# Rotary rotation in a Trainium2 decoder kernel: row blocks swapped by DMA inside SBUF instead of a TensorE permutation

## What is computed

```python
def rope(x, pos):                       # x: (..., 64)
    half = QK_ROPE // 2                 # 32
    ...
    x1, x2 = xf[..., :half], xf[..., half:]
    return jnp.concatenate([x1 * cos - x2 * sin, x2 * cos + x1 * sin], axis=-1)

cq = rms_norm(h @ w_dq, q_g)            # 1024 -> 512
q = (cq @ w_uq).reshape(n, t, N_HEADS, QK_NOPE + QK_ROPE)
q_pe = rope(q[..., QK_NOPE:], pos)
```

## Time and profile before

| | |
|---|---|
| median of 3 runs | 1427.34 us (1426.62 to 1427.58) |
| the profiled execution's own time | 1420.13 us |
| its span in the profile | 1417.3 us |
| granted TensorE clock, mean | 0.996 of full speed |
| TensorE busy | 1379.9 us, 97% of the span |
| VectorE busy | 890.2 us, 63% |
| ScalarE busy | 539.3 us, 38% |
| GpSimd busy | 176.0 us, 12% |

### The profile page before, as it was taken

How to read it: one execution, slowest core, us unless ns; L and a number is a source line. 1 busy time by engine, 2 the same in 40 slices (tenths; PEclk the granted TensorE clock), 3 DMA queues, 4 the chain that set the end, 5 groups by cost and what they waited for, 6 DMA issues and landing times.

```text
span 1417.3 us, 30501 instructions
## 1 busy us (share of the span) xinstructions
PE 1379.9 (97%) x11819; PEld 1303.4 (92%) x11819; DVE 890.2 (63%) x1516; ACT 539.3 (38%) x881; POOL 176.0 (12%) x339
## 2 busy tenths in 40 slices
PE   7999999999999999999999989999999999999998
PEld 6999999998999999999989955458999999999997
DVE  4444665226888888833366587674678888884334
ACT  5445444236332222233366132444642222223334
POOL 2000000000222222210000121100021222221000
PEclk9999999999999999999999999999999999999999
DMA  7432222222333333233333565301323333323322
GB/s 230 116 89 75 66 79 78 84 82 76 89 89 92 96 93 89 63 98 92 97 90 105 223 253 184 90 1 46 90 62 103 89 89 93 97 69 89 93 86 76
DMA packets 224442, 138.22 MB, mean 98 GB/s; under 512 B 12710, under 2 KB 220742, under 8 KB 223328
## 3 DMA queue, kind: packets, MB, share of 16 engines
q1 hardware_dynamic: 219688, 112.38, 27.6%
q0 software_dynamic: 4512, 24.69, 4.6%
q10 hardware_dynamic: 168, 0.11, 0.0%
HBM read 133.84 MB, written 3.67 MB: 97 GB/s over the span
## 4 chain that ended last, share of the span: by engine, by line
PE 90%; DVE 4%; ACT 3%; issue 2%; DMA 0%; ACTq 0%; DVEq 0%
PE psum L698 77%; PE psum L1124 2%; PE psum L1256 1%; PE psum L1281 1%; PE psum L1107 1%; PE psum L1085 1%; PE psum L889 1%; DVE kt L2175 1%; PE psum L1259 1%; DVE x L1838 1%; DVE ut L1832 1%; PE psum L875 1%; PE psum L1270 0%; ACT xh L1467 0%; DMA xs<-in_x_prompt 0%
## 5 line engine op out<-in xcount | busy, mean ns | idle before, releaser
L1794 DVE TENSOR_TENSOR wl<-ws,wh 128x1024 fp32r<-128x1024 f32 x214 | 262.0, 1224 | 318.0 <-ACT wh L1341 175.9
L698 PE MATMUL psum<-xh,wh 128*128 128x260 f32 x2032 | 418.6, 285 | 3.4 <-DVE xl L1813 2.7
L698 PE MATMUL psum<-xh,wl 128*128 128x260 f32 x2032 | 415.0, 283 | 0.0
L698 PE MATMUL psum<-xl,wh 128*128 128x260 f32 x2032 | 414.5, 283 | 0.0
L698 PEld LDWEIGHTS psum<-xh,wh 128*128 128x128 f32 x2032 | 316.3, 189 | 6.0 <-issue 3.0
L698 PEld LDWEIGHTS psum<-xh,wl 128*128 128x128 f32 x2032 | 316.0, 189 | 0.0
L698 PEld LDWEIGHTS psum<-xl,wh 128*128 128x128 f32 x2032 | 315.3, 189 | 0.1
L1341 ACT ACTIVATE wh<-ws 128x1024 fp32r<-128x1024 f32 x144 | 152.0, 1056 | 300.4 <-PE psum L698 300.4
L698 PE MATMUL psum<-acth,wh 128*128 128x260 f32 x704 | 145.3, 284 | 0.0
L698 PE MATMUL psum<-acth,wl 128*128 128x260 f32 x704 | 144.1, 282 | 0.0
L698 PE MATMUL psum<-actl,wh 128*128 128x260 f32 x704 | 144.0, 282 | 0.0
(11 more groups left out here) (321 smaller groups left out, 1805.8 us busy)
## 6 DMA issues: line engine op xcount, KB each, us to landing
ws<-in_w_up SPq DMA_DIRECT2D x88, 512.0 KB, 3.8
ws<-in_w_in_a SPq DMA_DIRECT2D x32, 512.0 KB, 4.1
ws<-in_w_down SPq DMA_DIRECT2D x28, 384.0 KB, 3.4
ws<-in_w_down SPq DMA_DIRECT2D x32, 320.0 KB, 3.1
ws<-in_w_out_a SPq DMA_DIRECT2D x16, 512.0 KB, 3.8
ws<-in_w_o SPq DMA_DIRECT2D x8, 512.0 KB, 4.4
xn<-in_x_prompt SPq DMA_DIRECT2D x4, 512.0 KB, 7.8
ws<-in_w_dq SPq DMA_DIRECT2D x4, 512.0 KB, 5.5
```

Of the source, the lines that this page charges most:

```text
L698: mm = pe.matmul(psum[:, 2 * slot + b, 0:HB], w, r[:, k, b * HB:(b + 1) * HB], start=st, stop=en)
L1794: dve.tensor_tensor(low_, ws[:, slot4, :], f32(high), ALU.subtract).then_inc(w_low, 1)
```

## The change

The permutation by TensorE is gone. ScalarE starts transfers from SBUF to SBUF instead, four for each 128-row tile, each of 32 rows of 520 values (2080 bytes a row), from the block of rows beside the one it writes. The sign of the sine goes into the constant table. `rotate` multiplies the swapped copy by the signed sine in place and adds the product of the original with the cosine; all three of its operations now read SBUF. The sums for the query norm move from ahead of the first query tile to a place inside it, ahead of its last quarter. The mask `keep` takes the place of `perm` in the constants, which are 128 columns narrower.

```diff
-    for m in range(P):
-        d = m % ROPE
-
-        c[m + half if d < half else m - half, P + m] = -1.0 if d < half else 1.0
+    c[:, P:2 * P] = np.arange(P)[:, None] <= np.arange(P)[None, :]
...
-    c[:, 3 * P + T:3 * P + 2 * T] = np.tile(np.sin(ang), (4, 1))
+    c[:, 3 * P + T:3 * P + 2 * T] = np.tile(np.sin(ang), (4, 1)) * np.where(np.arange(P) % ROPE < half, -1, 1)[:, None]
...
 # TensorE
-            pe.wait_ge(evac_kv, 3)
-            for b in range(2):
-                mm = pe.matmul(psum[:, 4 + b, 0:HB], perm, krr[:, b * HB:(b + 1) * HB], start=True, stop=True)
-            mm.then_inc(rotk_done, 1)
-            rms("cq")
-
-            def turn_q(t):
...
                 for k in range(KQ):
                     if t == 0:
+                        if k == KQ - 1:
+                            rms("cq")
                         pe.wait_ge(cql_ready, k + 1)
...
-                if 4 <= t < 8:
-                    turn_q(t - 4)
                 if t == 10:
 
                     pe.wait_ge(d_uk, 16)
-                    pe.wait_ge(rotq_step, 8)
+                    pe.wait_ge(ln_done, SSB["cq"] + 1)
...
 # ScalarE
+            def swap_halves(dst, src, sent):
+
+                for lo in range(0, P, ROPE // 2):
+                    act.dma_start(dst[lo:lo + ROPE // 2, :], src[lo ^ (ROPE // 2):(lo ^ (ROPE // 2)) + ROPE // 2, :]).then_inc(sent, 16)
+
             roots()
             rms("kv", r2)
+            act.wait_ge(evac_kv, 3)
+            swap_halves(krt, krr, d_swapk)
...
             rms("cq", r2)
+            def swap_query(t):
+
+                act.wait_ge(evac_uq, t + 1)
+                wait(act, d_swapq[t % 2], 64 * (t // 2))
+                swap_halves(qr[:, t, :], qrr[:, t, :], d_swapq[t % 2])
+
             for j in range(-1, 4):
                 ahead_static(U_UQ + j)
+                if j < 2:
+                    for t in ((0,), (1, 2), (3,))[j + 1]:
+                        swap_query(t)
...
 # VectorE
-            def rotate(dst, raw_, rot, tmp, done, step, n):
-
-                dve.wait_ge(done, n + 1)
-                dve.tensor_tensor(halves(tmp), rot, halves(sin), ALU.mult)
-                dve.tensor_tensor(dst, raw_, cos, ALU.mult).then_inc(step, 1)
+            def rotate(dst, raw_, tmp, sem, value, step, n):
+
+                dve.wait_ge(sem, value)
+                dve.tensor_tensor(dst, dst, sin, ALU.mult)
+                dve.tensor_tensor(tmp, raw_, cos, ALU.mult).then_inc(step, 1)
...
-            rotate(krt[:, :], krr[:, :], psum[:, 4:6, 0:HB], ut[:, 0, :], rotk_done, rotk_step, 0)
+            rotate(krt[:, :], krr[:, :], ut[:, 0, :], d_swapk, 64, rotk_step, 0)
...
-                    rotate(qr[:, j, :], qrr[:, j, :], psum[:, 4 + 2 * (j % 2):6 + 2 * (j % 2), 0:HB], ut[:, j % 2, :], rotq_done, rotq_step, j)
+                    rotate(qr[:, j, :], qrr[:, j, :], ut[:, j % 2, :], d_swapq[j % 2], 64 * (j // 2 + 1), rotq_step, j)
```

More of the change, by code:

```diff
@@ L75 @@
 SSB = {n: sum(2 if m in ON_PE + HALVED else 1 for m, _, _ in GROUPS_SQ[:i]) for i, (n, _, _) in enumerate(GROUPS_SQ)}
-K_SELH = 4 * P + 2 * T + NS
+K_SELH = 3 * P + 2 * T + NS
 K_GRP = K_SELH + H
@@ L129, in constants @@
     c[:, 3 * P:3 * P + T] = np.tile(np.cos(ang), (4, 1))
-    c[:, 3 * P + T:3 * P + 2 * T] = np.tile(np.sin(ang), (4, 1))
+    c[:, 3 * P + T:3 * P + 2 * T] = np.tile(np.sin(ang), (4, 1)) * np.where(np.arange(P) % ROPE < half, -1, 1)[:, None]
     for r in range(NS * H):
         c[r, 3 * P + 2 * T + r // H] = 1.0
-    c[:, 3 * P + 2 * T + NS:4 * P + 2 * T + NS] = np.arange(P)[:, None] <= np.arange(P)[None, :]
     p = np.arange(P)
@@ L227, in trunk @@
         arena = top[0]
-        ident, perm = cst[:, 0:P], cst[:, P:2 * P]
+        ident, keep = cst[:, 0:P], cst[:, P:2 * P]
         cmask = cst[:, 2 * P:3 * P]
@@ L231, in trunk @@
         own = cst[:, 3 * P + 2 * T:3 * P + 2 * T + NS]
-        keep = cst[:, 3 * P + 2 * T + NS:4 * P + 2 * T + NS]
         selh, grp = cst[:, K_SELH:K_SELH + H], cst[:, K_GRP:K_GRP + GRP]
@@ L364, in trunk @@
         csT_done, csn_ready, csn_sent, m_ready = S("csT_done"), S("csn_ready"), S("csn_sent"), S("m_ready")
[L366 to L369, removed]
+        evac_kv, evac_dq, evac_uq, d_swapk, rotk_step, ck_step, ckt_ready = (S(n) for n in (
+            "evac_kv", "evac_dq", "evac_uq", "d_swapk", "rotk_step", "ck_step", "ckt_ready"))
+        cqh_ready, cql_ready, rotq_step = (S(n) for n in ("cqh_ready", "cql_ready", "rotq_step"))
+        d_swapq = [S(f"d_swapq{i}") for i in range(2)]
         ql_read, qlT_done, ols_ready, olpT_done, oss_ready, osT_done, own_low, narrow_clear = (S(n) for n in (
```

## The result

| | before | after |
|---|---|---|
| median, both kernels run in turn, 9 runs each | 1427.18 us (1425.13 to 1428.80) | 1430.97 us (1429.29 to 1432.92) |
| ratio | | 1.0028, 95% interval 1.0019 to 1.0037 |
| the profiled execution, its own time | 1420.13 us | 1432.09 us |
| its span | 1417.3 us | 1430.3 us |

The changed kernel is slower by 4.0 us (0.0028 x 1427), with 2.7 to 5.3 as the interval. 1428.0 was forecast, with 1425.2 to 1431.6 as the range. The time lies in the range, but beyond the 0.2% that the prediction counts as no change. So the forecast was 3.0 us too low, the measured time is 0.6 us inside the range's upper end, and the likeliest case (no change, 0.68) was not the one that came.

The account below looks back on a forecast made before the run. TensorE, busy 97% of the span, was taken to bound the kernel; it gets about 5 us ahead but gives it back before tile 10, which starts 0.7 us later: 1427.34 + 0.7 = 1428.0 us, range 1425.2 to 1431.6.

Parts of the forecast that it names:

- what is removed: TensorE's query tiles: five permutations, 4.35 us, plus a 0.91 us wait, 5.26 us; about 4.9 us gain after a 0.3 us wait.
- what comes late next: Before tile 10: weights of `U_UQ` + 5, queued behind the gathers, land at 805.2, so tile 10 starts at 810.2, 0.7 us later.
- the size of the swaps' addition: Weights of `U_UQ` + 5: swap bytes on the shared DMA engines, 2.5 us at 430 GB/s, delay their landing by 2.1 us.
- the bound of 5: Upper bound in us for the swaps' delay of the weights: twice the bytes' time, if 32-row blocks move at half rate.
- Rival C: DMA: transfers of 32 rows run at half rate, adding 5 us; tile 10 3.7 us later, 1431.0 us, slower; chance 0.08.
- ScalarE behind the swaps: ScalarE's queue: waits for swap landings hold later high parts; decides only if swap 1 lands past 797.2; 794.5 taken.
- rival B: ScalarE held by swaps, swap 1 landing at 800 to 803: tile 10 3.5 to 6.5 us later, about 1432; chance 0.13.
- The chain of 13.0: From swap 1's landing through ScalarE's starts, high and low parts, rotations and tile readings to tile 8's reading: 13.0 us together.
- D: Before tile 10: weights land early enough once TensorE asks earlier; full 4.9 us gain, 1422.4 us, faster; chance 0.11.
- A: Before tile 10: swaps cost the weights nothing, landing stays at 803.1; gain is the cap, 1.4 us, 1425.9; chance 0.18.

Follow-up runs that it names:

- e4: Changed kernel with one more wait: GpSimd starts the gathers only when the last query swap has landed; 1421.79 us against 1426.46, ratio to before 0.9965.
- e5: e3 with the gathers also held until query tile 4 is read; ratio to the kernel before 0.9974.
- e3: Changed kernel without its 20 swap transfers, the rotation reading unswapped rows (results not the reference's); ratio to the kernel before 1.0003.
- e8: As e7, but each query transfer moves 32 of 520 columns and the queries' rotation reads unswapped rows; ratio to the kernel before 1.0007.
- e9: e3 with ten filler matmuls on TensorE ahead of query tile 10, on another chip than most runs; ratio to the kernel before 0.9989.
- e1: The kernel before, profiled once more without any edit; one run, 1428.17 us.
- e7: Changed kernel with own semaphores for query swaps 2 and 3, so ScalarE starts them without waiting for swaps 0 and 1; ratio to before 1.0053.
- e6: The kernel before, with the gathers held until VectorE has read the fifth query tile, on another chip than most runs; ratio to before 1.0003.

## Why the prediction was right or wrong

**Right: what is removed.** 4.9 us were to be gained if nothing came late. e4 and e5 gain 4.95 and 4.94.

**Right: what comes late next.** That the weights of `U_UQ` + 5 set tile 10, that the permutations' gain is given back in front of it, and the order behind them: the high part at 806.67 + 5.0 gives 811.67; tile 10 starts at 811.61. The gathers started at 777.36, which is 779.34 with the shift of 1.98, as forecast. ScalarE's high part is released by the DMA, as was to be seen.

**Wrong: the size of the swaps' addition, "2.1, most of the full sum, since 430 GB/s is a busy state".** From the start of the stretch to the last high part it is 806.67 - 771.76 = 34.91 us. It is 29.36 before, where TensorE releases this high part, and 28.92 in e3, where the weights do. So the addition is 5.5 to 6.0 us. That is the term that was mis-sized, and it lies outside of the bound of 5.

Where it comes from is in the windows from the weights' start to their landing, 27.6 us after and 22.3 us in e3. The shares are means of 16 engines:

- The swaps' own packets are 12.1% of 27.6, 3.3 us.
- The gathers' 720 packets take 73.8% of 27.6 = 20.4 us, against 81.5% of 22.3 = 18.2 in e3 (and 79.1% of 23 = 18.2 before, window 779:802). They are 2.2 us slower beside the swaps.
- The weights' own packets take 7.9% of 27.6, against 7.9% of 22.3 in e3: 0.4 us more.

Together that is 6.0. In e8, with the same packets and a sixteenth of the bytes, nearly all of it is gone (29.34 against the 28.92 of e3). So two things were wrong. The swaps' rows were priced at the rate of the gathers, 2.5 us and 2.1 taken, and they took 3.3: 104 ns a row of 2080 bytes, 20 GB/s per engine, where a gather's packet of 15.4 KB took 577 ns, 27 GB/s. And what the swaps do to the packets of the other queues, 2.6 us, was put at nothing; it is the larger part. Why those packets get slower is open. In e4, where no gathers run, the rows' share is higher still, 31.3% x 16 x 14 us = 70 us of engine time, 137 ns a row or 15 GB/s per engine; that too is not explained.

Rival C had this size (5) and this time (1431.0), with a chance of 0.08. That its time was met is luck in part: it had all of the 5 us in the swaps' own rows at half the rate, where 3.3 were measured, and nothing for the clock. A cause for the rows' rate is not shown. The Trainium skill, "SBUF — State Buffer", "Door 1: The DMA port swizzle (why [64,N] ≈ [32,N])", has 32 neighbouring rows reach half of the ports. The 15 against 27 GB/s would fit that, but it would fit a general price of short rows between two places of SBUF as well. No run moved the same rows in another grouping, so this stays open.

**Missing: the clock.** No step of the prediction gave the idle time before tile 10 a price beyond its length. Before, the granted clock was 1.00 throughout; after, tile 10 took 4.39 us instead of 2.88. That is 1.5 us. e3 has the same (4.51), and e9 takes it away there. The sum of the stretch: tile 10 starts 39.85 us into it, against 35.75, 4.1 later (0.7 forecast, 3.4 from the larger addition), the tile is 1.5 longer, the rest 0.1: 5.7 together. The runs say 4.0 (2.7 to 5.3), so they do not bear out all of the 5.7 of this one profile. Against the profile of e1 the span is longer by 3.9 only; the changed kernel's trace reached the stretch 1.4 us earlier than that of e1. What share of the 5.7 a typical run has is open.

**Half right: ScalarE behind the swaps (rival B).** Swap 1 landed when the starts of swap 3 began, at 796.12, or 798.1 with the shift. 791 to 798 was the span given, 794.5 was taken, and 797.2 was the value from which it was to decide. The chain of 13.0 from there ends at 809.1, plus 0.75 since the starts took 0.61 each and not 0.42: 809.9. That is 1.7 us before the 811.6 that the weights set. By the clock of the earlier trace rows it is 811.9, 1.7 us later than the forecast's 810.2 and 2.4 later than before. So by this estimate, had the weights come as forecast, this chain would have set tile 10, and not they. The wait of swap 2 for swap 0, which had no price in the sum, made TensorE stand 3.65 us before tile 6; before tile 8, where some 2 us were foreseen, it was 1.26. e7 shows that these waits are not what costs in the changed kernel: with them gone the stretch is 1.2 us longer. No run has both the swaps beside the gathers and early weights, so what the chain would cost by itself is not measured.

**By my own marks.** Tile 10 was to start between 808 and 813: 811.61 + 1.98 = 813.59, past the mark, as the two missing terms made it. The weights were to take 22 to 24 us to land; they took 21.4 and 27.0, 24.2 in the median. The query swaps took 8.7 us (6 to 12), the key's 2.8 (2 to 3).

**Rivals.** D (the full gain) is out, and e4 shows what it was missing. A's cap of 1.4 is about the most that could come with the gathers where they are: e3 won 1.9 up to tile 10 and lost 1.6 to the clock, and only e9 keeps it (1.66).

The Trainium skill, "DMA: Bandwidth & Descriptors", "Queues, rings and completion order", has the engines go round the queues packet by packet. The 92 to 94 to 93 in three queues agree with it, with turns of one row or one completion of the trace. The prediction read turns of one from the 19.3 us to landing. That does not follow: at 9 to a turn in both queues, four turns of the gathers at 0.58 us a packet would be 21 us as well, an estimate with the 9 of that page. What speaks for turns of one is that the counts are equal in windows as short as 2 us, 46, 47 and 47 in 789:791, which is 3 on each engine.

## What to carry to other kernels

Before work is taken off the busiest engine, look how late the transfers are that feed it: here they landed 0.1 us ahead of need, so of the 4.9 us some 1.4 to 1.9 at most could be kept, until the competing gathers, for which nobody was waiting, started 14 us later. A transfer that replaces computation must be priced at what its own kind of row takes on the DMA engines and at how much it slows what runs there already, not at the best rate seen. And an idle time of TensorE costs more than its length when the granted clock falls behind it: read the clock by windows after each gap that a change opens.

## What the runs showed of the hardware that was not expected

- A transfer of 65 KB inside SBUF, a quarter of a swap, landed in 2.0 us (e4) to 2.8 us (the key's) without the gathers, in 8.7 us beside them, and in 14.3 us in e7, where more swaps are under way at once. Even the 4 KB pieces of e8 took 10.0 us beside the gathers, so most of that time is not their own bytes.
- From the weights' start to their landing the engines moved 325 GB/s with three queues at work and 359 before with two. The same 720 gather packets took 20.4 us of all engines' time beside the swaps and 18.2 without them.
- The start of a transfer took ScalarE 0.61 us in this stretch, against 0.26 to 0.59.
- Idle times of 2 to 4 us on TensorE were followed by products 0.43 us apart instead of 0.24; the idle time of 1.26 us before tile 8 was not. Small matmuls of 2.39 us in the gap kept the clock at 1.00 (e9).
- Two chips ran the kernel before at 1417.65 and 1426.5 us. In the profiles of e6 and e1, 3.4 us of the difference are at one wait and 6.1 behind it. No changed kernel was timed on both.
